# fp32r transposes of P, one pair later, from a copy that GpSimd issues

## The chip, the cores and the metric

One NeuronCore of a Trainium2 chip runs the whole program as one launch. The metric is the device time of that core in microseconds. The kernel before takes 1619.56 us, the median of three runs (1619.38 to 1620.76).

## What is computed

A transformer layer of 1024 tokens plus 16 meta tokens, model width 1024, all in float32: a mixer of retention (4 heads) and sliding-window attention (16 query heads, 4 key heads of 64), then an MLP of width 4096. The part that matters here is the attention over blocks of 128 queries. Each block sees 16 meta keys, the block before and its own; each head has a sink that takes part in the softmax alone.

```python
def block(args):
    qn, kn, vn, n = args
    ...
    keys = jnp.concatenate([k_meta, kn], axis=1)
    vals = jnp.concatenate([v_meta, vn], axis=1)
    scores = (jnp.einsum('bqhgd,bkhd->bhgqk', qn, keys).astype(jnp.float32)
              - slopes * dist.astype(jnp.float32))
    scores = jnp.where(valid, scores, -jnp.inf)
    m = jnp.maximum(jnp.max(scores, axis=-1, keepdims=True), sink)
    p = jnp.exp(scores - m)
    probs = p / (jnp.sum(p, axis=-1, keepdims=True) + jnp.exp(sink - m))
    return jnp.einsum('bhgqk,bkhd->bqhgd', probs.astype(vals.dtype), vals)
```

## The kernel before

Every engine has its own program, written out by hand; semaphores join them. Large products are split in a high and a low part of type fp32r and done as three matmuls (high x high, high x low, low x high: lines 1084, 1088, 1089). ScalarE casts the high part of each weight tile (WH), VectorE subtracts for the low part (WL, L2172).

The attention is the stage from about 461 to 728 us. Its work is cut into 64 pairs of heads: block n = pair // 8, heads 2p and 2p + 1 with p = pair % 8. It is a software pipeline of STEPS = 67 steps T. TensorE fills the steps with the gate projection (`gate_step`, 3 or 4 triples of matmuls a step), so that it has work while a pair goes through the other engines. A pair's way:

- TensorE, step T: `scores(T)` (L1370), two matmuls of 272 columns (144 in block 0) for each of the two heads, into banks 2 and 3.
- VectorE: `top(T)` (L2630) adds the distance term, writes to PR and finds the maxima NM. PR has three buffers, T % 3, of 546 columns: a sink column, the 272 keys of each head, a sink column.
- ScalarE: the exponential, in place in PR, with its sum in RS (L1932). VectorE: RC = 1 / RS (L2663).
- GpSimd: PR times RC (L959), one instruction for each head; it also writes the two sink columns of the pair to come (`set_sink`, L940).
- TensorE, step T + 2: `transpose_p` (L1384, and L1387 for the meta keys): five transposes of 128 columns from PR, type fp32, to banks 4 and 6; three in block 0. They stand ahead of that step's scores, and ahead of the transposes of the next block's queries and keys (L1419, L1427), which are of type fp32r already.
- ScalarE casts the bank to PTH (L1909), VectorE's `lo_p` makes PTL (L2638) and, every second pair, PTM (L2642). `lo_p` of the pair of two steps ago stands ahead of `top(T)` in VectorE's program.
- TensorE, every second step: `values(G)` for two pairs (L1402, L1406); ScalarE copies the result to YA, SP writes one half of it to RT and GpSimd adds the other (L980, accumulating transfers).

GpSimd's queue also stores the gate tiles (L884), loads KV (L893) and the distances (L968). An instruction that issues a transfer waits for its semaphores in the queue, with all that stands behind it.

Of the kernel before, what the change touches and what calls it, by code (L numbers as in the profile page):

```python
# [14 lines left out]
P = 128  # L15
# [48 lines left out]
STEPS = NPAIR + 3  # L64
# [64 lines left out]
KV_FREE = {4: (6, 7), 5: (0, 7), 6: (0, 1)}  # L129
# [78 lines left out]
def build(nc, x, meta, g_mix, w_in, g_ret, g_q, g_k, sinks, w_ret, w_swa, w_out, g_mlp, w_up, w_down,  # L208
          c_ident, c_mask, c_cols, c_dist, x_ch, g_ch, out):
    with ExitStack() as ctx:  # L210
# [92 lines left out]
        KV = at("KV", O_M, [NB, SL])  # L303
        KVR = at("KVR", O_M, [NB, SL], F32R)
        MKV = at("MKV", O_M + 16384, [SL])
        MVB = at("MVB", O_M + 18432, [2, 4 * P], F32R)
        KST = at("KST", O_M + 22528, [2, 4, P], F32R)
        KNF = at("KNF", O_M + 26624, [256])
        PTH = at("PTH", O_M + 27776, [2, 4, P], F32R)
# [3 lines left out]
        RSW = at("RSW", O_M + 31872, [NB, 20])  # L313
# [8 lines left out]
        YA = [at("YA0", O_V + 30208, [SL]), at("YA1", O_M + 16384, [SL])]  # L322
        YA2 = at("YA2", O_M + 22528, [SL])
# [58 lines left out]
        def kv_half(tile, n, c):  # L382

            return tile[:, n, :].rearrange("p (g c d) -> p g c d", g=4, c=2)[:, :, c, :]
# [194 lines left out]
        GS0, CF0, MU0 = 4, 48, 64  # L579

        raw_aside = [*xb_full, *yc_done]

        def raw_block(slab, k):
# [6 lines left out]
            if k in (4, 5) and slab in KV_FREE:  # L590
                return KV[:, KV_FREE[slab][k - 4], :]
# [14 lines left out]
        def _(sp):  # L606
# [84 lines left out]
            for T in range(STEPS):  # L691
# [3 lines left out]
                elif T == 23:  # L695
                    sp.wait_ge(pv_full, 8)
                    sp.wait_ge(w_ready, wn(SLAB_D + 1, 5) + 1)
                    load_aside(SLAB_D + 2)
                elif T == 41:
                    sp.wait_ge(pv_full, 12)  # L700
# [102 lines left out]
        def _(pool):  # L803
# [139 lines left out]
            pool.wait_ge(d_set, 1)  # L943
            set_sink(0)
# [6 lines left out]
            for T in range(STEPS + 2):  # L951
                if T + 1 < NPAIR:
                    set_sink(T + 1)
                if 1 <= T <= NPAIR:
# [21 lines left out]
                if T >= 6 and T % 2 == 0:  # L976
                    G = (T - 6) // 2
# [100 lines left out]
        def _(pe):  # L1078
# [281 lines left out]
            def scores(T):  # L1360
                n, p = T // 8, T % 8
                g = p // 2
                if p % 2 == 0:
                    pe.wait_ge(aqT_rdy, 4 if n == 0 else 4 * n + g + 1)
                    pe.wait_ge(akT_rdy, 4 if n == 0 else 4 * n + g + 1)
                for hl in range(2):
                    if T >= 1:
                        pe.wait_ge(nm_rdy, 2 * (T - 1) + hl + 1)
                    for part in range(2):
                        mm = pe.matmul(B[2 + hl][:, 0:NKEY if n else NKEY0], QT[:, 2 * p + hl, :], KTS[:, part, g, keys_of(n, hl)],  # L1370
                                       start=part == 0, stop=part == 1)
                    mm.then_inc(sc_full, 1)

            def transpose_p(pair):
                n, b = pair // 8, pair % 3
                pe.wait_ge(pn_rdy, pair + 1)
                if pair >= 1:
# [1704 lines left out]
```

## Time and profile before

| | |
|---|---|
| median of three runs | 1619.56 us |
| lowest, highest | 1619.38, 1620.76 us |
| span of the profiled execution | 1618.2 us, 22594 instructions |
| busy over the span | TensorE 99%, VectorE 64%, ScalarE 48%, GpSimd 27% |

The page gives the profiled execution's span, from its first to its last instruction; no time of its own for the whole execution stands beside it, so the 1.3 us between span and median hold what lies around the span and the difference from run to run. A row of the timeline reads: start in us from the span's start, duration, engine, line, operation, output <- inputs, shapes, count of merged instructions, and in brackets how long the engine had been idle and who released it. PE is TensorE's matmuls, PEld its weight loads, DVE VectorE, ACT ScalarE, POOL GpSimd. Matmuls are pipelined: the distance from start to start is what one costs. A row of POOL begins when the instruction is handed over, so behind a running one its duration holds the wait.

### The profile page before, as it was taken

What the parts mean: (1) busy time and instruction counts of PE and PEld (TensorE: products, weight loads), DVE (VectorE), ACT (ScalarE), POOL (GpSimd) and SP (SyncE); (2) the same over time, 40 slices, a digit from 0 to 9 for tenths busy, and PEclk for the clock granted to TensorE, in tenths of its full rate; (3) what the DMA queues carried; (4) which work ended last, traced back from release to release, by engine and by line L of the source; (5) the groups of instructions that cost most, each with busy time, mean ns of one, the idle gap of its engine ahead of it and who ended that gap; (6) DMA issues with size and microseconds to landing.
All of it is one profiled execution on the core that took longest, in us unless ns stands there. A gap on an engine that the chain in (4) does not pass through costs nothing.

```text
span 1618.2 us, 22594 instructions
## 1 busy us (share of the span) xinstructions
PE 1610.1 (99%) x7984; PEld 1347.5 (83%) x7984; DVE 1030.6 (64%) x1913; ACT 769.9 (48%) x1567; POOL 437.1 (27%) x675
## 2 busy tenths in 40 slices
PE   9999999999999999999999999999999999999999
PEld 6888888888888888888888888888888888888887
DVE  6775556655657676757565338866665657766675
ACT  6533334545547676763222126655545544444442
POOL 1101010221359888875221000121111122100000
PEclk9999999999999999999999999999999999999999
DMA  8323232645424343438553223344444399733452
GB/s 289 116 98 117 95 124 72 232 166 186 162 88 114 84 94 83 106 82 262 164 202 104 72 65 124 129 170 150 149 144 148 119 321 356 239 98 98 149 183 92
DMA packets 119599, 236.53 MB, mean 146 GB/s; under 512 B 13904, under 2 KB 48128, under 8 KB 119488
## 3 DMA queue, kind: packets, MB, share of 16 engines
q0 software_dynamic: 45904, 126.93, 23.6%
q1 hardware_dynamic: 73440, 108.03, 21.6%
q8 instruction: 64, 1.05, 0.3%
q14 instruction: 47, 0.39, 0.1%
q10 hardware_dynamic: 144, 0.13, 0.0%
HBM read 157.05 MB, written 69.47 MB: 140 GB/s over the span
## 4 chain that ended last, share of the span: by engine, by line
PE 97%; DVE 1%; DMA 1%; ACT 0%; SPq 0%; POOL 0%; issue 0%; DVEq 0%; ACTq 0%
PE bank L1084 29%; PE bank L1089 29%; PE bank L1088 29%; PE bank L1370 2%; PE bank L1402 2%; PE bank L1384 2%; PE bank L1419 0%; PE bank L1127 0%; PE bank L1502 0%; PE bank L1288 0%; PE bank L1406 0%; PE bank L1452 0%; DMA PX<-in_w_in 0%; PE bank L1387 0%; DVE WL L2172 0%; PE bank L1427 0%
## 5 line engine op out<-in xcount | busy, mean ns | idle before, releaser
L1084 PE MATMUL bank<-WH,ADH 128*128 128x512 f32 x448 | 174.3, 389 | 0.0
L1088 PE MATMUL bank<-WH,ADL 128*128 128x512 f32 x448 | 174.3, 389 | 0.0
L1089 PE MATMUL bank<-WL,ADH 128*128 128x512 f32 x448 | 174.3, 389 | 0.0
L1084 PE MATMUL bank<-HN,WH 128*128 128x512 f32 x384 | 152.4, 397 | 0.0
L2098 ACT CAST ADH<-ARAW 128x512 fp32r<-128x512 f32 x112 | 69.5, 621 | 169.9 <-PE bank L1089 160.9
L1089 PE MATMUL bank<-HN,WH 128*128 128x512 f32 x384 | 150.3, 391 | 0.0
L1088 PE MATMUL bank<-HN,WL 128*128 128x512 f32 x384 | 150.0, 391 | 0.0
L959 POOL TENSOR_SCALAR PR<-PR,RC 128x272 f32<-128x272 f32 (+1 forms) x128 | 131.0, 1099 | 44.9 <-DVE RC L2663 44.4
L2917 DVE TENSOR_TENSOR ADL<-ARAW,ADH 128x512 fp32r<-128x512 f32 x112 | 77.5, 692 | 96.9 <-ACT ADH L2098 96.7
L1084 PE MATMUL bank<-SOPH,WH 128*128 128x512 f32 x256 | 99.8, 390 | 0.0
L1089 PE MATMUL bank<-SOPL,WH 128*128 128x512 f32 x256 | 99.6, 389 | 0.0
L1088 PE MATMUL bank<-SOPH,WL 128*128 128x512 f32 x256 | 99.6, 389 | 0.0
L1088 PEld LDWEIGHTS bank<-WH,ADL 128*128 128x128 f32 x448 | 84.1, 188 | 17.6
L1089 PEld LDWEIGHTS bank<-WL,ADH 128*128 128x128 f32 x448 | 84.1, 188 | 17.4
L1084 PEld LDWEIGHTS bank<-WH,ADH 128*128 128x128 f32 x448 | 84.1, 188 | 17.4
L1932 ACT ACTIVATE PR<-PR,NM 128x273 f32<-128x273 f32 (+1 forms) x128 | 64.4, 506 | 50.1 <-DVE NM L2630 50.1
L1089 PEld LDWEIGHTS bank<-HN,WH 128*128 128x128 f32 x384 | 72.0, 188 | 15.8
L1084 PE MATMUL bank<-WH,HN 128*128 128x512 f32 x208 | 82.7, 397 | 1.1 <-DVE WL L2172 0.7
L1084 PEld LDWEIGHTS bank<-HN,WH 128*128 128x128 f32 x384 | 72.3, 188 | 12.3 <-issue 0.3
L1088 PEld LDWEIGHTS bank<-HN,WL 128*128 128x128 f32 x384 | 72.3, 188 | 11.9
L1089 PE MATMUL bank<-WL,HN 128*128 128x512 f32 x208 | 81.1, 390 | 0.0
L1088 PE MATMUL bank<-WH,HN 128*128 128x512 f32 x208 | 81.0, 390 | 0.0
(356 smaller groups left out, 4242.8 us busy)
## 6 DMA issues: line engine op xcount, KB each, us to landing
ARAW<-uop SPq DMA_DIRECT2D x112, 256.0 KB, 3.0
uop<-US POOLq DMA_DIRECT2D x64, 256.0 KB, 2.8
WRAW<-in_w_up SPq DMA_DIRECT2D x15, 1024.0 KB, 6.2
RAW<-in_w_in SPq DMA_DIRECT2D x58, 256.0 KB, 4.0
gates<-TB POOLq DMA_DIRECT2D x48, 256.0 KB, 2.4
uop<-UA POOLq DMA_DIRECT2D x48, 256.0 KB, 3.1
proj<-SA POOLq DMA_DIRECT2D x36, 256.0 KB, 2.5
RT<-proj POOLq DMA_DIRECT2D x8, 1024.0 KB, 8.8
```

The source lines that it names most:

```text
L959: pr = pool.tensor_scalar(keys, keys, RC[:, b, hl:hl + 1], None, ALU.mult)
L1084: mm = pe.matmul(bank, ahi, bhi, start=first, stop=False, skip_group_check=onto)
L1088: pe.matmul(bank, alo, bhi, start=False, stop=False, skip_group_check=onto)
L1089: return pe.matmul(bank, ahi, blo, start=False, stop=last, skip_group_check=onto)
L1370: mm = pe.matmul(B[2 + hl][:, 0:NKEY if n else NKEY0], QT[:, 2 * p + hl, :], KTS[:, part, g, keys_of(n, hl)], start=part == 0, stop=part == 1)
L1384: pe.transpose(B[4][:, c * P:(c + 1) * P], PR[:, b, key:key + P], IDN[:, :])
L1402: pe.matmul(B[7][:, :], v, tile[:, sl, :, :].rearrange("p h t -> p (h t)"), start=opens, stop=True, skip_group_check=not opens)
L1932: e = act.activation(part, part, ACT.Exp, scale=-1.0, bias=NM[:, T % 3, hl:hl + 1], accum_out=RS[:, T % 3, hl:hl + 1])
L2098: act.copy(ADH[:, n % 4, :], ARAW[:, n % 4, :]).then_inc(da_hi, 1)
L2917: dve.tensor_tensor(ADL[:, n % 4, :], ARAW[:, n % 4, :], ADH[:, n % 4, :].bitcast(F32), ALU.subtract)\
```

## The change

PW is a new tile of two buffers, type fp32r. When GpSimd has scaled pair T - 1 it issues a transfer within SBUF that copies the 544 key columns of PR to PW (144 x 2 in block 0); its waits are its own scaling (`pn_rdy`) and the transposes of the pair two before (`pt_full`). TensorE transposes from PW, in type fp32r with the fp32r identity IDR, at step T + 3 (LAG = 3), one transpose behind each score matmul and the fifth behind the last. Values, and the high and low parts of P, move a step later with it; STEPS is 68. The sink columns are written by VectorE, just ahead of the maxima, once the copy of the pair that used the buffer has landed. To make room, KV keeps four blocks instead of eight, loaded later, and two RAW blocks lie in an area of their own, RAWA, so SP loses two waits.

```diff
+LAG = 3
-STEPS = NPAIR + 3
+STEPS = NPAIR + LAG + 1
...
-KV_FREE = {4: (6, 7), 5: (0, 7), 6: (0, 1)}
+ASIDE = (4, 5, 6)
+NKV = 4
...
-        KV = at("KV", O_M, [NB, SL])
+        KV = at("KV", O_M, [NKV, SL])
+        RAWA = at("RAWA", O_M + 8192, [2, SL])
+        PW = at("PW", O_M + 12288, [2, 2 * NKEY], F32R)
...
-                if T >= 4 and T % 2 == 0:
-                    G = (T - 4) // 2
+                if T >= LAG + 2 and T % 2 == 1:
+                    G = (T - LAG - 2) // 2
                     sp.wait_ge(ya_rdy, G + 1)
...
-            def set_sink(T):
-
-                if T >= 3:
-                    pool.wait_ge(e_rdy, T - 2)
-                p = T % 8
-                first, second = sink_at(T // 8, 0), sink_at(T // 8, 1)
-                pool.tensor_copy(PR[:, T % 3, first:second + 1:second - first], NSK[:, 2 * p:2 * p + 2]).then_inc(sk_set, 1)
+            def copy_p(pair):
+
+                n, b = pair // 8, pair % 2
+                lo, hi = (0, 2 * NKEY) if n else (P, P + 2 * NKEY0)
+                if pair >= 2:
+                    pool.wait_ge(pt_full, pair - 1)
+                pool.wait_ge(pn_rdy, pair + 1)
+                pool.dma_start(PW[:, b, lo:hi].bitcast(F32), PR[:, pair % 3, 1 + lo:1 + hi]).then_inc(pw_full[b], 16)
...
                     pr.then_inc(pn_rdy, 1)
+                    copy_p(T - 1)
...
-                if T in (5, 13, 21, 37):
-                    n = min(T // 8, 3)
-                    pool.wait_ge(qh_rdy, 3 * n + 3 if n else 2)
+                if T % 8 == 4 and 2 <= T // 8 < 6:
+                    n = T // 8 - 2
+                    pool.wait_ge(pv_full, 4 * (n + 2))
                     pool.wait_ge(qf_rdy, n + 2)
-                    if n >= 2:
-                        pool.wait_ge(w_ready, wn(SLAB_D + n - 1, 5) + 1)
-                    load_kv(n + 4)
+                    load_kv(n + NKV)
...
+            def transpose_p(pair, c):
+                n, b = pair // 8, pair % 2
+                if c == 0:
+                    pe.wait_ge(pw_full[b], PW0[b] + 16 * (pair // 2 + 1))
+                    if pair >= 1:
+                        pe.wait_ge(pl_rdy, split_of(pair - 1))
+                    else:
+                        pe.wait_ge(aqT_rdy, 4)
+                if c == 4:
+                    if pair % 2 == 0 and pair >= 2:
+                        pe.wait_ge(pl_rdy, meta_of(pair // 2 - 1))
+                    pe.transpose(B[6][:, (pair % 2) * P:(pair % 2 + 1) * P].bitcast(F32R),
+                                 PW[:, b, 2 * P:3 * P], IDR[:, :]).then_inc(pt_full, 1)
+                elif c // 2 in slots_of(n):
+                    key = pr_slot(n, c % 2, c // 2) - 1
+                    pe.transpose(B[4][:, c * P:(c + 1) * P].bitcast(F32R), PW[:, b, key:key + P], IDR[:, :])
...
-                if T >= 4 and T % 2 == 0:
-                    values((T - 4) // 2)
-                if 2 <= T < NPAIR + 2:
-                    transpose_p(T - 2)
+                if T >= LAG + 2 and T % 2 == 1:
+                    values((T - LAG - 2) // 2)
...
-                if T < NPAIR:
-                    scores(T)
+                for i in range(5):
+                    if T < NPAIR and i < 4:
+                        score(T, i)
+                    if LAG <= T < NPAIR + LAG:
+                        transpose_p(T - LAG, i)
...
                 if T >= 3:
-                    dve.wait_ge(pt_full, T - 2)
+                    dve.wait_ge(pw_full[(T - 3) % 2], PW0[(T - 3) % 2] + 16 * ((T - 3) // 2 + 1))
+                if T == 0:
+                    dve.wait_ge(d_set, 1)
+                first, second = sink_at(n, 0), sink_at(n, 1)
+                dve.tensor_copy(PR[:, T % 3, first:second + 1:second - first], NSK[:, 2 * p:2 * p + 2]).then_inc(sk_set, 1)
```

`score(T, i)` is one of the four matmuls of `scores(T)`, with the same waits.

TensorE, the middle of the stage (step 27, fourth block), before: the gate's matmuls, then the transposes of pair 25 from PR, then the four scores of pair 27.

```order
L1089 MATMUL bank<-HN,WH 128x512
L1384 MATMUL bank<-IDN,PR 128x128 [waits pl_rdy,pn_rdy]
L1384 MATMUL bank<-IDN,PR 128x128 x3
L1387 MATMUL bank<-IDN,PR 128x128
L1370 MATMUL bank<-KTS,QT 128x272 [waits nm_rdy]
L1370 MATMUL bank<-KTS,QT 128x272
L1370 MATMUL bank<-KTS,QT 128x272 [waits nm_rdy]
L1370 MATMUL bank<-KTS,QT 128x272
L1084 MATMUL bank<-HN,WH 128x512
```

The same step of the change (the semaphore named c_full is one of the two that PW's copies count on, which are shared with earlier uses):

```order
L1406 MATMUL bank<-PTM,MVB 128x2x128
L1368 MATMUL bank<-KTS,QT 128x272 [waits nm_rdy]
L1388 MATMUL bank<-IDR,PW 128x128 [waits pl_rdy,c_full]
L1368 MATMUL bank<-KTS,QT 128x272
L1388 MATMUL bank<-IDR,PW 128x128
L1368 MATMUL bank<-KTS,QT 128x272 [waits nm_rdy]
L1388 MATMUL bank<-IDR,PW 128x128
L1368 MATMUL bank<-KTS,QT 128x272
L1388 MATMUL bank<-IDR,PW 128x128
L1384 MATMUL bank<-IDR,PW 128x128 [waits pl_rdy]
L1084 MATMUL bank<-HN,WH 128x512
```

The transposes, of pair 24 now, stand behind one score each, the last two next to each other; this step now has the values ahead of them.

GpSimd at about the same steps, before:

```order
L940 COPY PR<-NSK 128x2 [waits e_rdy]
L959 TENSOR_SCALAR PR<-PR,RC 128x272 [waits rc_rdy]
L959 TENSOR_SCALAR PR<-PR,RC 128x272
L884 DMA gates<-TB 128x512 [waits a_free]
L980 DMA RT<-YA_154 64x2x128 [waits yc_done0]
L980 DMA RT<-YA_154 64x2x128
```

and of the change, over two steps, in one of which KV is loaded:

```order
L960 TENSOR_SCALAR PR<-PR,RC 128x272 [waits rc_rdy]
L960 TENSOR_SCALAR PR<-PR,RC 128x272
L945 DMA PW<-PR 128x544 [waits pn_rdy,pt_full]
L980 DMA RT<-YA_156 64x2x128 [waits yc_done0]
L980 DMA RT<-YA_156 64x2x128
L960 TENSOR_SCALAR PR<-PR,RC 128x272 [waits rc_rdy]
L960 TENSOR_SCALAR PR<-PR,RC 128x272
L945 DMA PW<-PR 128x544 [waits pn_rdy,pt_full]
L897 DMA KV<-proj 128x4x64 [waits qf_rdy,pv_full]
L897 DMA KV<-proj 128x4x64
```

The sink copy is gone and the copy of P stands right behind the scaling, ahead of the step's other transfers.

## Rows read from the trace of the kernel before

**Rows 1.** The page: busy time and share of each engine; TensorE's clock by slice.

```profile
PE 1610.1 (99%) x7984; PEld 1347.5 (83%) x7984; DVE 1030.6 (64%) x1913; ACT 769.9 (48%) x1567; POOL 437.1 (27%) x675
...
PEclk9999999999999999999999999999999999999999
```

**Rows 2.** The chain of waits that ended last, by engine.

```profile
PE 97%; DVE 1%; DMA 1%; ACT 0%; SPq 0%; POOL 0%; issue 0%; DVEq 0%; ACTq 0%
```

**Rows 3.** Busy us by engine in the attention stage, 461 to 728, eight stretches summed.

```profile
sum 267.00, PE 266.52 PEld 231.75 DVE 183.84 ACT 183.76 POOL 219.13; mean PE 33.31 PEld 28.97 DVE 22.98 ACT 22.97 POOL 27.39
```

**Rows 4.** Groups of TensorE instructions: the transposes of P, busy us, mean ns.

```profile
L1384 PE MATMUL bank<-IDN,PR 128*128 128x128 f32 x240 | 36.7, 273 | 0.5 <-POOL PR L959 0.5
...
L1387 PE MATMUL bank<-IDN,PR 128*128 128x128 f32 x64 | 17.4, 273 | 0.0
```

**Rows 5.** Timeline of TensorE's matmuls, one step.

```profile
566.31 0.60 PE L1384 MATMUL bank<-IDN,PR 128*128 128x128 f32 x4
566.75 0.27 PE L1387 MATMUL bank<-IDN,PR 128*128 128x128 f32 x1
...
567.36 0.39 PE L1084 MATMUL bank<-HN,WH 128*128 128x512 f32 x1
```

**Rows 6.** Timeline of weight loads, fp32r transposes of queries.

```profile
453.69 1.42 PEld L1337 LDWEIGHTS bank<-IDR,QST 128*128 128x128 f32 x16 [0.54 <-DVE KTS L2589]
455.06 0.19 PEld L1084 LDWEIGHTS bank<-HN,WH 128*128 128x128 f32 x1
```

**Rows 7.** Timeline of weight loads, fp32r matmuls of 128 columns.

```profile
303.42 1.08 PEld L1288 LDWEIGHTS bank<-QTR,KTR 128*128 128x128 f32 x8
304.43 0.19 PEld L1084 LDWEIGHTS bank<-HN,WH 128*128 128x128 f32 x1
```

**Rows 8.** Groups of GpSimd instructions in the stage, 461 to 728.

```profile
L980 POOL DMA_DIRECT2D RT<-YA x60 | 61.6, 1227 | 0.0
L940 POOL COPY PR<-NSK 128x2 f32<-128x2 f32 x63 | 43.6, 693 | 0.0
...
L893 POOL DMA_DIRECT2D KV<-proj x8 | 7.6, 1121 | 0.0
```

**Rows 9.** Lines 884 and 980 in the stage: ns min/median/max, then landing from issue.

```profile
L884 POOL DMA_DIRECT2D gates<-TB x26: 612/636/1365, 468.1 to 719.0; - x26
...
DMA to landing us min/median/max: 2.4/2.7/4.8
...
L980 POOL DMA_DIRECT2D RT<-YA x60: 972/1330/2174, 482.1 to 723.7; - x60
...
DMA to landing us min/median/max: 2.5/3.2/6.3
```

**Rows 10.** Timeline of all engines, pair 31 on its way, and step 32.

```profile
584.47 0.27 PE L1387 MATMUL bank<-IDN,PR 128*128 128x128 f32 x1
...
584.71 0.73 PE L1370 MATMUL bank<-KTS,QT 128*128 128x272 f32 x4
...
586.57 0.50 DVE L2630 CUSTOM_DVE_ANT_0 PR<-bank,DT,NSK 128x272 f32<-128x272 f32 x1
...
588.60 1.91 POOL L959 TENSOR_SCALAR PR<-PR,RC 128x272 f32<-128x272 f32 x2 [1.88 <-DVE RC L2663]
...
588.92 0.27 PE L1387 MATMUL bank<-IDN,PR 128*128 128x128 f32 x1
...
590.46 0.49 DVE L2630 CUSTOM_DVE_ANT_0 PR<-bank,DT,NSK 128x272 f32<-128x272 f32 x1
...
597.48 0.74 PE L1370 MATMUL bank<-KTS,QT 128*128 128x272 f32 x4
```

**Rows 11.** Timeline of VectorE and GpSimd, a scaling behind weight splits, a sink copy.

```profile
567.85 1.27 DVE L2172 TENSOR_TENSOR WL<-RAW,WH 128x512 fp32r<-128x512 f32 x2
...
568.03 2.79 POOL L959 TENSOR_SCALAR PR<-PR,RC 128x272 f32<-128x272 f32 x2
...
570.78 0.18 POOL L940 COPY PR<-NSK 128x2 f32<-128x2 f32 x1
```

More of the change, by code:

```diff
@@ L579, in build @@
         GS0, CF0, MU0 = 4, 48, 64
+        pw_full, PW0 = [c_full, mu_full], [CF0 + 48, MU0 + 64]
         raw_aside = [*xb_full, *yc_done]
@@ L1358, in _, with score @@
                     ahead[i]()
-            def scores(T):
-                n, p = T // 8, T % 8
+            def score(T, i):
+                n, p, hl, part = T // 8, T % 8, i // 2, i % 2
                 g = p // 2
-                if p % 2 == 0:
+                if p % 2 == 0 and i == 0:
                     pe.wait_ge(aqT_rdy, 4 if n == 0 else 4 * n + g + 1)
                     pe.wait_ge(akT_rdy, 4 if n == 0 else 4 * n + g + 1)
[L1366 to L1371, printed above, removed]
-                    mm.then_inc(sc_full, 1)
@@ L1374, in transpose_p @@
[L1374 to L1377, printed above, removed]
-                    pe.wait_ge(pl_rdy, split_of(pair - 1))
-                else:
-                    pe.wait_ge(aqT_rdy, 4)
-                for sl in slots_of(n):
-                    for hl in range(2):
-                        c, key = 2 * sl + hl, pr_slot(n, hl, sl)
-                        pe.transpose(B[4][:, c * P:(c + 1) * P], PR[:, b, key:key + P], IDN[:, :])
-                if pair % 2 == 0 and pair >= 2:
-                    pe.wait_ge(pl_rdy, meta_of(pair // 2 - 1))
-                pe.transpose(B[6][:, (pair % 2) * P:(pair % 2 + 1) * P],
-                             PR[:, b, 1 + 2 * P:1 + 3 * P], IDN[:, :]).then_inc(pt_full, 1)
+                if T >= 1 and part == 0:
+                    pe.wait_ge(nm_rdy, 2 * (T - 1) + hl + 1)
@@ new lines, in score @@
+                mm = pe.matmul(B[2 + hl][:, 0:NKEY if n else NKEY0], QT[:, 2 * p + hl, :], KTS[:, part, g, keys_of(n, hl)],
+                               start=part == 0, stop=part == 1)
+                if part == 1:
+                    mm.then_inc(sc_full, 1)
+            def transpose_p(pair, c):
[14 more added lines that the diff above has]
+                    pe.transpose(B[4][:, c * P:(c + 1) * P].bitcast(F32R), PW[:, b, key:key + P], IDR[:, :])
@@ L1941, in _ @@
                         g.then_inc(a_free if c < 16 else th_rdy, 1)
-                if 2 <= T < NPAIR + 2:
-                    take_p(T - 2)
-                if T >= 4 and T % 2 == 0:
-                    take_y((T - 4) // 2)
+                if LAG <= T < NPAIR + LAG:
+                    take_p(T - LAG)
+                if T >= LAG + 2 and T % 2 == 1:
+                    take_y((T - LAG - 2) // 2)
                 if T % 8 == 2 and T // 8 + 1 < NB:
@@ L2675, in _ @@
                         split_lo(slab, k)
-                if T > NPAIR:
+                if T > NPAIR + 1:
                     for slab, k in new_slabs(T):
                         split_lo(slab, k)
-                if T >= NPAIR and T < NPAIR + 2:
+                if NPAIR + 1 <= T < NPAIR + 3:
                     for b in range(4):
-                        lo_ys(4 * (T - NPAIR) + b, b, T - NPAIR)
-                splits = new_slabs(T) if T < NPAIR else []
+                        lo_ys(4 * (T - NPAIR - 1) + b, b, T - NPAIR - 1)
+                splits = new_slabs(T) if T <= NPAIR else []
                 if T % 8 == 0 and T // 8 + 1 < NB:
```

52 lines of the change are left out of this document (23 added, 29 removed).

## The prediction

> **What bounds the kernel now.** I read the page's busy shares first, then the chain of waits, then the busy time by stretch. TensorE is busy 99% of the span and the clock row shows 9 in every slice, so the granted clock never falls [rows 1]. The chain that ended last is 97% TensorE [rows 2]. In the stage that the change touches, 461 to 728 us, TensorE is busy 266.52 of 267 us, while GpSimd is busy 219.13, VectorE 183.84 and ScalarE 183.76 [rows 3]. So nothing is won unless TensorE itself does less, and anything that makes TensorE wait there costs its full length. The second thing to see is that GpSimd is at 82% of that stage already; no other helper is nearly so full. The sum is made against the span of the profiled execution, 1618.2 us; the median of the runs is 1.3 us above it, which I add at the end. A measurement of this kernel can tell a change from none at about 0.2%, 3.2 us.
>
> **TensorE's own work.** The change touches 240 + 64 = 304 transposes [rows 4]. Five of them and the four score matmuls of a step are seen in [rows 5]: four transposes from 566.31 to 566.75, 0.109 us each; the whole group of nine takes 567.36 - 566.31 = 1.05, so 5 x 0.109 leaves 0.125 for a score matmul of 272 columns. What an fp32r transpose costs next to another is in [rows 6]: 16 weight loads from 453.69 to the next load at 455.06, 0.0855 each. That looks like 304 x 0.0235 = 7.1 us. But the new order doesn't put them next to each other. It puts four of the five behind a score matmul, with another score matmul behind each. What counts is then which of matmul and following weight load is the longer. The weight load of an ordinary fp32r matmul is in [rows 7]: eight from 303.42 to 304.43, of which the first sat behind a matmul of 512 columns (0.23), so 0.78 / 7 = 0.111 each, although those matmuls have only 128 columns. A transpose streams 128 columns too, so it can't cover the 0.111 of the score matmul's load behind it. Score, transpose: 0.125 as now, the load of the transpose is hidden. Transpose, score: 0.111, where the fp32 transpose costs 0.109. Only the fourth transpose, followed by the fifth, gets 0.0855. So a group of nine falls from 1.05 to about 1.02. That is 0.024 x 56 pairs with five transposes, 1.3 us; the eight pairs of the first block (three transposes) and the last three pairs, which have no scores beside them, bring 0.4. Together **-1.7 us**. The transposes of the next block's queries and keys keep their neighbours: 0.
>
> The page "TensorE: Matmul & The Clock Gate" of the Trainium skill (section on LDWEIGHTS) gives a load as columns / 1.2, 107 ns for 128 columns, for every kind. The trace agrees for the ordinary load (0.111) and not for the transposes (0.0855). By that rule alone a transpose would cost 0.107 everywhere and this term would be -0.6 us instead of -1.7; the measured rows decide.
>
> **GpSimd.** Removed: 64 copies of two sink columns, about 0.2 us each by their shortest (0.18, [rows 11]); the 43.6 us of [rows 8] is mostly waiting behind transfers that are still being issued. Added: 64 issues of a transfer of 128 rows of 2176 bytes. The nearest row is the gate store, 128 rows of 2048 bytes, 0.636 us [rows 9]; the other end is the accumulating transfer of y, 1.03 us for each of a pair ([rows 8]: 61.6 us over 60). I take the gate store, nearly the same shape. 219.1 - 64 x 0.2 + 64 x 0.63 = 246.6 us of 267, 92%. By itself that still fits, with 0.3 us to spare in a mean step of 4.17 us. But its work is bunched: a step with scaling (1.9), P's copy (0.63), two y transfers (2.06) and a gate store (0.63) is 5.2 us, and in four steps two loads of KV of about 1 us each come on top (7.6 us over 8, [rows 8]), in others the distances. It then falls 1 to 3 us behind and catches up by 0.3 a step. Copying to PW also waits for the transposes of two pairs earlier; those end about 5.2 us after the pair's own scores began, when its scaling ends as well, so I cost that at nothing. Behind that wait stand the gate stores and the y transfers; their readers are many us away.
>
> **From the scores to the copy.** Now the scores of pair 31 start at 584.71, 0.24 behind the last transpose of that step, VectorE's maxima at 586.57, the scaling runs 588.60 to 590.51 [rows 10]. After the change the last transpose of a step starts some 0.9 us after the first score instead of 0.24 before it, and ScalarE's cast and VectorE's low part stand ahead of the maxima, so these and all behind move by about 1.15: scaled at 591.7. Landing is 2.7 us from the issue (gate store, median; 2.4 to 4.8 [rows 9]): 594.4. TensorE wants it behind the first score three steps on, 597.48 + 0.12 [rows 10]. Slack 3.2 us, less what GpSimd is behind. Where 1 to 3 us of lateness meet a landing in its upper half, it is gone, and what is late next is P. I count six such places (the KV loads, the block ends, the last pairs, where steps are shorter and no score covers the wait), 0.5 us each: **+3.0 us**. Bounds: 0, if landings stay at 2.4 to 2.7 (TensorE waits for P 0.5 us once today [rows 4]); 13, if every copy is late by 0.2. VectorE's added copy (under 0.2 us as on GpSimd) hides in its 83 idle us. The maxima free the score banks: in a step without PTM's low part they started 590.46 - 588.92 = 1.54 after the last transpose [rows 10], so the first is done 0.9 + 1.54 + 0.5 = 2.95 after the first score, and the next scores come no earlier than 3.3 (1.02 for the group, nine gate matmuls at 0.23, two transposes of keys). Fits by 0.35; I put +0.2 there. The KV and RAW buffers move, with loads several steps ahead of use: 0. SP loses two waits: 0. The gate's matmuls are spread over 68 steps instead of 67, same count: 0.
>
> Sum: 1618.2 - 1.7 + 3.0 + 0.2 = 1619.7, and 1.3 to the median: **1621.0 us**.
>
> **Rivals.**
> (a) *The transposes get their cheap rate after all.* If a score's load can be drawn further ahead than behind the transpose, all 304 cost 0.0855 or less, and P arrives in time: 1619.6 - 7.1 = 1612.5. For it: the queue of loads isn't fully visible. Against it: in [rows 7] no load was ever hidden behind a shorter matmul. And an even shorter step would find GpSimd full. Chance 0.12.
> (b) *GpSimd becomes the bound: slower.* It decides when an issue of P's copy costs over (265 - 206.3) / 64 = 0.92 us, with 265 for the stage less 1.7 and 206.3 for GpSimd's work without the sinks. At the 1.03 of the y transfers it is 206.3 + 65.9 = 272.2 us of work in a stage of 265, 7 us over, and some 2 us of waits for RC that it can't fill: 1621 - 3 + 9, about 1628. For: it is the y transfers that share the queue. Against: the gate store's shape. 0.15.
> (c) *Landings come late.* The new transfers add some 17 MB (278 KB a pair) to the queue that carries y, gates and KV, and the y transfers already show a median of 3.2 and a worst of 6.3 us from issue [rows 9]. One copy in four late by 0.7 is 16 x 0.7 = 11 us in place of 3: about 1628. Related: the scaling takes 2.79 us instead of 1.91 when it starts while VectorE splits weights [rows 10, 11]. Chance 0.21. [...]
> (d) *It does nothing visible*: work and waits both near 0, 1619.6. This lies inside the forecast.
>
> **How the numbers follow.** Forecast with (d), 0.52; (a) 0.12; (b) 0.15; (c) 0.21. Faster by over 0.2% is (a) and a sliver of the forecast, 0.13; slower (b) and (c), 0.36; within 0.2% 0.51. The range takes the forecast's bounds, both slow rivals and the near edge of (a): 1614 to 1630. The forecast's own range is 1617 to 1623.
>
> **What would show it.** Right: a group of four scores and five transposes at about 1.02 us, with some 0.11 from each transpose to the score behind it; GpSimd near 245 us in the stage; its issue of P's copy about 0.63; a few TensorE waits on P's transfer, 3 us together; maxima 1 us later in their step. Wrong: groups of 0.95 or less (a), issues near 1 us and GpSimd without idle time (b), waits on the transfer in every other step (c), or waits of the scores for the maxima in most steps, which I hold for nearly free.

## The result, and the profile after

The changed kernel takes **1661.88 us**, the median of four runs (1660.92 to 1662.71), against 1619.47 for the kernel before in the same runs: a ratio of 1.0258, interval 1.0243 to 1.0272. It is 42 us slower where 1621.0 was forecast, and beyond every rival. The profiled execution took 1662.05 us for a span of 1660.1.

The page of the changed kernel: busy time and share, TensorE's busy tenths in 40 slices, and the chain that ended last.

```profile
PE 1620.5 (98%) x7984; PEld 1352.3 (81%) x7984; DVE 1039.0 (63%) x1977; ACT 771.7 (46%) x1567; POOL 472.2 (28%) x675
...
PE   9999999999999888899999999999999999999999
...
PE 87%; POOL 7%; DMA 3%; issue 1%; DVE 1%; ACT 0%; SPq 0%; POOLq 0%; DVEq 0%
```

The holes lie in the attention stage alone, and GpSimd, which had no part in the chain before [rows 2], has 7% of it now. The stage by stretches (length, busy us of TensorE, its weight loads, VectorE, ScalarE, GpSimd, then the granted clock, DMA share, GB/s), cut so that the sum covers the stage to its new end:

```profile
461.00:494.00 33.00, 33.00 (x191) 28.27 (x189) 22.22 (x82) 22.32 (x68) 20.19 (x30) 1.00 0.43 125
494.00:527.00 33.00, 29.42 (x171) 25.17 (x171) 19.05 (x65) 19.35 (x53) 28.59 (x34) 1.00 0.49 132
527.00:560.00 33.00, 28.66 (x171) 24.66 (x170) 19.43 (x63) 18.96 (x50) 28.49 (x33) 1.00 0.49 124
560.00:593.00 33.00, 25.95 (x138) 21.91 (x137) 21.51 (x61) 19.82 (x50) 29.30 (x31) 0.90 0.54 144
...
659.00:692.00 33.00, 26.42 (x144) 22.48 (x143) 22.20 (x63) 19.25 (x50) 28.17 (x31) 0.90 0.53 146
...
sum 309.00, PE 276.23 PEld 235.91 DVE 192.70 ACT 185.95 POOL 256.59; mean PE 30.69 PEld 26.21 DVE 21.41 ACT 20.66 POOL 28.51
```

Against [rows 3] the stage takes 309 us where it took 267: 42 us, the whole loss. TensorE idles 309 - 276.2 = 33 us in it (0.5 before), and is busy 276.2 - 266.5 = 10 us longer for work that should be shorter; two stretches show a granted clock of 0.90. The waits of this stage (engine and line, what it waited for: us, times, longest):

```profile
ACT PTH L1910 <- PE bank L1384: 70.0, 58, 4.3
...
PE bank L1388 <- DMA PW<-PR: 31.2, 19, 4.2
POOL PW L945 <- POOL PR L960: 30.8, 52, 0.8
...
POOL PR L960 <- DVE RC L2668: 9.2, 8, 3.3
POOL PW L945 <- PE bank L1384: 7.5, 12, 0.8
...
POOL gates L888 <- DVE TB L2663: 3.3, 1, 3.3
...
PE bank L1368 <- DVE NM L2635: 0.9, 2, 0.7
```

TensorE's missing 31 us are waits for the copy of P. GpSimd used to be idle until the reciprocals came (44.4 us, 38 times, in the same view of the kernel before); now only 9.2, 8 times. In its place stands an idle time that didn't exist: 30.8 + 7.5 = 38.3 us ahead of its own copy, 64 times. GpSimd's account closes on the stage: 256.6 busy + 38.3 + 9.2 + 3.3 = 307.4 of 309. Of the 9.2 us, 8.2 lie before 494 us, in the first block; behind it GpSimd has nearly nothing left. GpSimd's groups in the stage (count | busy us, mean ns | idle before; the mean holds time queued behind another issue), and six of its rows (start, us):

```profile
L945 POOL DMA_DIRECT2D PW<-PR x64 | 39.4, 615 | 38.4 <-POOL PR L960 30.8 <-PE bank L1384 7.5
L888 POOL DMA_DIRECT2D gates<-TB x27 | 15.3, 567 | 3.6 <-DVE TB L2663 3.3
```

```profile
599.09 1.75 POOL L960 TENSOR_SCALAR PR<-PR,RC 128x272 f32<-128x272 f32 x1
601.44 0.64 POOL L945 DMA_DIRECT2D PW<-PR  x1 [0.60 <-POOL PR L960]
602.11 1.92 POOL L960 TENSOR_SCALAR PR<-PR,RC 128x272 f32<-128x272 f32 x2
604.70 0.61 POOL L945 DMA_DIRECT2D PW<-PR  x1 [0.67 <-POOL PR L960]
605.31 0.55 POOL L888 DMA_DIRECT2D gates<-TB  x1
605.85 2.09 POOL L980 DMA_DIRECT2D RT<-YA  x2
```

The scaling ends at 602.11 + 1.92 = 604.03 and the copy starts at 604.70, though the copy's other wait, for the transposes, was satisfied by then. The gate store behind it, whose own wait (`a_free`) is satisfied too, follows at once. So the issue is 0.62 us as forecast, and the pair pays (39.4 + 38.4) / 64 = **1.22 us**. The views of issues give the copy's landing as 2.0/2.4/5.4 us (minimum, median, maximum): not late by itself.

### The profile page after: what moved, and what is told of

Same layout as the page of the kernel before. It is cut to its first block, busy times and chain, and to the rows that moved or that the text cites. A ratio compares the mean times of both kernels' runs of the same rounds, so it can differ in the third digit from the quotient of the medians.

```text
span 1660.1 us, 22666 instructions
## 1 busy us (share of the span) xinstructions
PE 1620.5 (98%) x7984; PEld 1352.3 (81%) x7984; DVE 1039.0 (63%) x1977; ACT 771.7 (46%) x1567; POOL 472.2 (28%) x675
## 4 chain that ended last, share of the span: by engine, by line
PE 87%; POOL 7%; DMA 3%; issue 1%; DVE 1%; ACT 0%; SPq 0%; POOLq 0%; DVEq 0%
PE bank L1084 27%; PE bank L1089 27%; PE bank L1088 27%; POOL PR L960 4%; DMA PW<-PR 2%; POOL RT L980 2%; PE bank L1368 1%; POOL PW L945 1%; PE bank L1402 1%; PE bank L1388 1%; PE bank L1127 0%; PE bank L1503 0%; PE bank L1288 0%; PE bank L1453 0%; DMA XR<-in_x 0%
## 5 line engine op out<-in xcount | busy, mean ns | idle before, releaser
L1084 PE MATMUL bank<-HN,WH 128*128 128x512 f32 x384 | 159.0, 414 | 0.4 <-DVE WL L2173 0.4
L960 POOL TENSOR_SCALAR PR<-PR,RC 128x272 f32<-128x272 f32 (+1 forms) x128 | 152.2, 1427 | 10.2 <-DVE RC L2668 9.2
L1089 PE MATMUL bank<-HN,WH 128*128 128x512 f32 x384 | 151.7, 395 | 0.0
L2643 DVE TENSOR_TENSOR PTL<-bank,PTH 128x512 fp32r<-128x512 f32 (+1 forms) x64 | 42.0, 657 | 80.8 <-ACT PTH L1910 80.8
L1089 PEld LDWEIGHTS bank<-HN,WH 128*128 128x128 f32 x384 | 73.0, 190 | 16.4
L1388 PE MATMUL bank<-IDR,PW 128*128 128x128 f32 x240 | 54.2, 232 | 31.3 <-DMA PW<-PR 31.2
L1088 PEld LDWEIGHTS bank<-HN,WL 128*128 128x128 f32 x384 | 73.6, 192 | 12.2
L1084 PE MATMUL bank<-WH,HN 128*128 128x512 f32 x208 | 82.7, 397 | 0.8 <-DVE WL L2173 0.3
```

The source lines that it names most:

```text
L960: pr = pool.tensor_scalar(keys, keys, RC[:, b, hl:hl + 1], None, ALU.mult)
L1084: mm = pe.matmul(bank, ahi, bhi, start=first, stop=False, skip_group_check=onto)
L1088: pe.matmul(bank, alo, bhi, start=False, stop=False, skip_group_check=onto)
L1089: return pe.matmul(bank, ahi, blo, start=False, stop=last, skip_group_check=onto)
L1388: pe.transpose(B[4][:, c * P:(c + 1) * P].bitcast(F32R), PW[:, b, key:key + P], IDR[:, :])
L2643: dve.tensor_tensor(pair_part(PTL, n, pair), pair_bank(n), pair_part(PTH, n, pair).bitcast(F32), ALU.subtract)\
```

## The experiments

**Theories.** A: GpSimd's time is the loss; a transfer that has to wait for GpSimd's own scaling costs it a start as well as the issue, 1.22 us a pair, and GpSimd is full. Rivals: the later place of the transposes and their order among the scores; VectorE's sink columns; landings and the DMA queue; the delivery of P itself.

The ratios below are to the kernel before as measured beside each run, with medians from 1620.11 to 1620.86 us.

### sp_copy: the copy on another queue

The call leaves GpSimd's loop, where it stood behind the scaling, and ends SyncE's step, with the same two waits; its landing is counted on two other semaphores.

```diff
-                    copy_p(T - 1)
...
+                if 1 <= T <= NPAIR:
+                    copy_p(T - 1)
```

> The changed kernel with one edit: the copy of P to PW is issued by SP, at the end of its step, with the same waits; GpSimd keeps scaling, y, gates and KV. Theory GPSIMD (its queue is the bound: 0.60 us of idling on its own scaling and 0.62 us of issue for each pair, 78 us of its 308): the stage falls back to 264 to 267 us and the time to 1616 to 1622. Theory LANDING (P arrives late because the transfer is slow or queued behind others): still 1640 or more, with waits of the transposes on the transfer. Theory VECTOR (the sink copies and the later maxima hold everything up): stays near 1660.

Measured: 1641.99 us (1640.27 to 1642.32), ratio 1.0132 (1.0117 to 1.0147). GpSimd is free again: it waits for reciprocals, 75.7 us in the stage, 39 times. That gives 20 of the 42 us back, not all of them as theory A had it; 1640 or more with waits on the transfer is what the rival of late landings expected. The waits of TensorE for P are 12.2 us now, 8 of them, and three of these are holes of over 3 us. One of them, in the timelines of SyncE's queue, GpSimd and TensorE:

```profile
488.21 2.14 POOL L962 TENSOR_SCALAR PR<-PR,RC 128x144 f32<-128x144 f32 x2
```

```profile
489.97 0.51 SPq L704 DMA_DIRECT2D PW<-PR  x1
495.92 0.93 SPq L689 DMA_DIRECT2D RAW<-in_w_in  x2
496.95 0.50 SPq L704 DMA_DIRECT2D PW<-PR  x1
```

```profile
501.37 0.37 PE L1389 MATMUL bank<-IDR,PW 128*128 128x128 f32 x1 [3.55 <-DMA PW<-PR]
```

The pair scaled at 488.21 to 490.35 is the one after that copied at 489.97 (a copy is issued only when its scaling is over). It was issued at 496.95, 6.6 us late, behind two weight loads of SyncE's step at 495.92, which wait for VectorE to split the blocks they overwrite. TensorE stood 3.55 us for it. The transposes began 501.37 - 496.95 = 4.4 us behind the issue, a slow landing beside the 3.1 in the median; with the 6.6 us back it would still have been in time.

### sp_grouped: with the transposes side by side

```diff
-                for i in range(5):
-                    if T < NPAIR and i < 4:
-                        score(T, i)
-                    if LAG <= T < NPAIR + LAG:
-                        transpose_p(T - LAG, i)
+                if LAG <= T < NPAIR + LAG:
+                    for i in range(5):
+                        transpose_p(T - LAG, i)
+                if T < NPAIR:
+                    for i in range(4):
+                        score(T, i)
```

(on top of sp_copy)

> As sp_copy, and the five transposes of a step stand together ahead of the four scores, not one behind each. By the weight loads (0.0855 us between transposes, 0.111 only for the last one, where each transpose ahead of a score now costs 0.111) a group of nine falls from 1.02 to 0.95: 0.07 x 61 pairs = 4 us less than sp_copy, 1612 to 1617. Rival: the order is worth nothing, the same time as sp_copy within 1 us.

Measured: 1631.74 us (1630.56 to 1633.95), ratio 1.0068 (1.0051 to 1.0085): 10 us below sp_copy, where 4 were expected, with three large holes still there. So the order costs, in a kernel where P is late as well; how much, the runs with P in time show further down.

### own_wait: the wait alone

The kernel before, and GpSimd waits for its own scaling; no copy.

```diff
                     pr.then_inc(pn_rdy, 1)
+                    pool.wait_ge(pn_rdy, T)
```

> The kernel before, with one added instruction: after each scaling GpSimd waits for its own scaling to be complete. No transfer of P, nothing else changed. If waiting for its own last instruction costs GpSimd 0.6 us by itself, the idle time ahead of the sink copy or the next transfer is 0.5 to 0.6 us in 64 places, GpSimd is at 219 + 38 = 257 of 267 us and the time rises by 0 to 8 us. If the 0.6 us belongs to the issue of a transfer alone, the idle time appears only where a transfer comes next, and the time stays at 1619 to 1621.

Measured: 1619.77 us (one run). GpSimd's waits in the stage:

```profile
POOL PR L959 <- DVE RC L2664: 22.4, 26, 3.1
...
POOL gates L884 <- POOL PR L959: 8.4, 26, 0.5
POOL RT L981 <- POOL PR L959: 6.6, 19, 0.5
```

The idle time comes up in front of transfers, 8.4 / 26 = 0.32 us each for the gate stores; the sink copies that follow such a wait directly, which are computing instructions, start 0.06 us behind it. Here GpSimd had idle time to pay with: its waits for reciprocals fell from 44.4 us to 22.4.

### copy_behind: the copy after the step's other transfers

Still on GpSimd, but behind the step's gate stores and y transfers.

```diff
-                    copy_p(T - 1)
...
+                if 1 <= T <= NPAIR:
+                    copy_p(T - 1)
```

> The changed kernel with the copy of P behind the step's other transfers (gates, distances, KV, y) in GpSimd's program, not ahead of them. Theory GPSIMD: in the steps that have another transfer (about five in eight) the wait for the scaling is covered, so some 0.6 x 40 = 24 us of idling go, and P lands 1 to 3 us later: 1635 to 1650. Theory LANDING: P later by 1 to 3 us makes it worse, over 1665.

Measured: 1645.85 us (one run). The idle time in front of the copy fell from 30.8 to 10.8 us (18 times, where no other transfer covers it), the time by 16. GpSimd has 26.9 us of waits for reciprocals again, and TensorE still waits 16.4 us for P, which now comes later.

### sp_first: SyncE's copy at the head of its step

```diff
             for T in range(STEPS):
+                if 1 <= T <= NPAIR:
+                    copy_p(T - 1)
...
-                if 1 <= T <= NPAIR:
-                    copy_p(T - 1)
```

> sp_copy with one thing moved: SyncE issues the copy of P at the head of its step, ahead of the weight and y transfers of that step, not behind them. Theory A (in sp_copy the copies at the changes of slab were queued on SyncE behind weight loads that wait for VectorE's splits, which are what made the three gaps of 3 to 4 us and the stretches at a granted clock of 0.90 to 0.95 around them): the gaps of 3.55, 3.38 and 3.17 us go, every stretch shows 0.98 or more, and the time falls from 1642 by the 10 us of gaps and some 8 of clock to 1620 to 1626. Theory B (the copy is late because the scaling itself is late, VectorE's reciprocals standing behind its split work at those places): the gaps stay within 1 us of what they were and the time stays at 1638 to 1643. A new cost could come up: the weight loads now wait behind the copy, which waits for the scaling; then VectorE would show waits for RAW blocks.

Measured: **1623.09 us** (1621.63 to 1624.17), ratio 1.0012 (1.0003 to 1.0022). TensorE's waits for P are 0.2 us in the whole stage. The same stretch of sp_copy and of sp_first:

```profile
494.00:527.00 33.00, 29.20 (x156) 24.83 (x156) 18.70 (x63) 17.47 (x47) 23.31 (x26) 0.90 0.45 124
```

```profile
494.00:527.00 33.00, 32.15 (x190) 27.58 (x189) 21.96 (x73) 20.84 (x57) 27.13 (x29) 1.00 0.55 145
```

With the hole the granted clock is 0.90 and 156 matmuls get done, without it 1.00 and 190. The new wait that was feared (weight loads behind the copy) doesn't show. So everything above 1623 in the changed kernel comes from which queue issues the copy, and when: 1661.9 - 1623.1 = 39 us.

### lag_only and sinks_dve: the rest of the change, without the copy

lag_only keeps the later place, the order among the scores, the smaller ring of KV and VectorE's sink columns, with fp32 transposes straight from PR:

```diff
-                    pe.wait_ge(pw_full[b], PW0[b] + 16 * (pair // 2 + 1))
+                    pe.wait_ge(pn_rdy, pair + 1)
...
-                    pe.transpose(B[4][:, c * P:(c + 1) * P].bitcast(F32R), PW[:, b, key:key + P], IDR[:, :])
+                    pe.transpose(B[4][:, c * P:(c + 1) * P], PR[:, pair % 3, key:key + P], IDN[:, :])
```

> The changed kernel without the copy of P: the transposes are plain fp32 again and read P itself, but a pair later and between the scores, and the sink columns are VectorE's; the ring of four K/V buffers, the aside buffers and the odd steps of y stay too. If the loss of the change is the copy's alone (GpSimd's transfer issues and the waits behind them): within 4 us of before, 1616 to 1624. If the later place or VectorE's sink columns carry a part of it: that part shows here, up to 1645.

Measured: 1622.88 us (1622.09 to 1624.62), ratio 1.0011 (1.0002 to 1.0021): 2 us of the 42.

sinks_dve is the kernel before with `set_sink` moved from GpSimd into VectorE's `top`.

> The kernel before with the sink columns written by VectorE ahead of the maxima and by nothing else. VectorE gets 64 copies of 0.2 to 0.4 us, GpSimd loses 64 of 0.2 us. By the prediction +0.2 us; if the maxima come so much later that TensorE's scores wait, 2 to 10 us more.

Measured: 1619.67 us (one run). No cost; VectorE's 63 copies are 12.9 us of busy time beside TensorE's work.

### lag_group and sp_first_group: order and kind

The grouping of sp_grouped on top of lag_only and of sp_first.

> lag_only with the five plain fp32 transposes together ahead of the scores. Against sp_first_group it differs in the kind of transposes alone (and the copy that fp32r needs). If the rate of a weight load of fp32r transposes next to each other is what sp_first_group won: 1615.9 + 304 x 0.0235 = 1623. If it won by the order, with the kind of no weight: 1616 to 1618.

> sp_grouped (the five transposes together ahead of the scores) with the copy at the head of SyncE's step. A: sp_grouped's 1632 less its gaps of 3.2, 4.7 and 5.3 us and the lower clock around them, 1613 to 1618, which is below the 1619.5 of before. B: stays at 1628 to 1633.

Measured: lag_group 1618.31 us (1617.36 to 1619.09), ratio 0.9988 (0.9978 to 0.9997); sp_first_group **1615.92 us** (1615.43 to 1617.08), ratio 0.9970 (0.9958 to 0.9982), faster than both kernels. Grouping alone, with the plain fp32 kind, is 1.9 us of that (lag_group). The four kernels differ in the order and in the kind (with the copy that fp32r needs), and one step without values of each shows them on TensorE's timeline. Grouped fp32, grouped fp32r, alternating fp32, alternating fp32r:

```profile
502.99 0.63 PE L1378 MATMUL bank<-IDN,PR 128*128 128x128 f32 x4
...
504.07 0.39 PE L1074 MATMUL bank<-HN,WH 128*128 128x512 f32 x1
504.30 0.39 PE L1078 MATMUL bank<-HN,WL 128*128 128x512 f32 x1
```

```profile
503.69 0.51 PE L1389 MATMUL bank<-IDR,PW 128*128 128x128 f32 x4
504.03 0.25 PE L1385 MATMUL bank<-IDR,PW 128*128 128x128 f32 x1
...
504.70 0.40 PE L1085 MATMUL bank<-HN,WH 128*128 128x512 f32 x1
504.93 0.40 PE L1089 MATMUL bank<-HN,WL 128*128 128x512 f32 x1
```

```profile
503.78 0.36 PE L1358 MATMUL bank<-KTS,QT 128*128 128x272 f32 x1
...
504.00 0.38 PE L1358 MATMUL bank<-KTS,QT 128*128 128x272 f32 x1
...
504.83 0.47 PE L1074 MATMUL bank<-HN,WH 128*128 128x512 f32 x1
505.14 0.39 PE L1078 MATMUL bank<-HN,WL 128*128 128x512 f32 x1
```

```profile
504.95 0.36 PE L1369 MATMUL bank<-KTS,QT 128*128 128x272 f32 x1
505.15 0.22 PE L1389 MATMUL bank<-IDR,PW 128*128 128x128 f32 x1
505.21 0.34 PE L1369 MATMUL bank<-KTS,QT 128*128 128x272 f32 x1
505.39 0.22 PE L1389 MATMUL bank<-IDR,PW 128*128 128x128 f32 x1
505.45 0.34 PE L1369 MATMUL bank<-KTS,QT 128*128 128x272 f32 x1
...
505.99 0.46 PE L1085 MATMUL bank<-HN,WH 128*128 128x512 f32 x1
506.29 0.40 PE L1089 MATMUL bank<-HN,WL 128*128 128x512 f32 x1
```

From the first of the nine to the second gate matmul (the first is drawn long after a transpose): 1.31, 1.24, 1.36, 1.34 us; over all groups of nine in the stage that are followed by a gate matmul and have no idle time (some fifty in each kernel) the means are 1.30, 1.22, 1.36 and 1.33. Side by side the fp32r kind is worth 0.07 here; alternating it is worth 0.02. In the last fence score to score is 505.45 - 505.21 = 0.24 us: 0.18 to the transpose and 0.06 back. The alternating order costs 0.05 for fp32 and 0.10 for fp32r. In run times the fp32r kind wins nothing alternating (1623.1 against 1622.9 for fp32, within the spread) and 2.4 us grouped (1615.9 against 1618.3), where I had expected 7 from 304 x 0.0235. TensorE is busy 4.9 us less in that run (1604.6 against 1609.5 over the span); its waits for P, 1.7 us in three places, are a part of what was lost again. The order is worth 4.6 us for fp32 and 7.2 for fp32r. Where lag_group is one side of a difference, the kernels before differ by 0.6 us, so 4.6 may be 4.0 and 2.4 may be 3.0.

### extra, extra_two, extra_wait: GpSimd's price by itself

sp_first, where P arrives by SyncE, and GpSimd issues one or two transfers more a pair which nothing reads, from a tile that nothing changes. The first added line stands in extra_wait alone, the third in extra_two alone.

```diff
                     pr.then_inc(pn_rdy, 1)
+                    pool.wait_ge(pn_rdy, T) 
+                    pool.dma_start(spare[T - 1], HN[:, 0, 0, 0:2 * NKEY].bitcast(F32)).then_inc(c_full, 16)
+                    pool.dma_start(spare[NPAIR + T - 1], HN[:, 0, 0, 0:2 * NKEY].bitcast(F32)).then_inc(c_full, 16)
```

> sp_first (SyncE copies P) plus one more transfer a pair that nothing reads, issued by GpSimd right behind its scaling: 128 rows of 2176 bytes from a tile that nothing changes to a spare place in memory. It waits for nothing. GpSimd is busy 209.5 of 267 us in sp_first's stage; 64 x 0.62 makes 249, so by both theories it still fits and the time stays within 5 us of sp_first's 1623. If queues and landings were what the copy on GpSimd spoils, this run would already be slow (over 1630).

> As extra, with two such transfers a pair and no wait: 1.24 us of issue a pair. If what counts is GpSimd's time alone, wherever it comes from, this is as slow as extra_wait (1643 to 1662); by the prediction's own bound an issue cost over 0.92 us a pair makes GpSimd the limit. If the wait hurts in another way (the order of releases), this one stays near 1625.

> As extra, but GpSimd first waits for the semaphore of its own scaling, as the copy of P has to. Theory A (a transfer's issue that waits for the scaling can't begin under it and starts 0.6 us behind its end, so the pair costs 1.22 us of GpSimd instead of 0.62): 209.5 + 64 x 1.22 = 288 us of work for a stage of 267, so the stage grows by 20 us or more and the time is 1643 to 1662. Theory B (the issue's 0.62 is all that counts and the change lost elsewhere): the same time as extra.

Measured: extra 1630.67 us (1628.11 to 1631.24), ratio 1.0062 (1.0045 to 1.0079); extra_wait 1650.30 (1647.65 to 1652.49), 1.0181 (1.0166 to 1.0196); extra_two 1657.88 (1655.75 to 1659.44), 1.0228 (1.0213 to 1.0243). One pair of extra and one of extra_two on GpSimd's timeline, then the transfer's group in extra_wait:

```profile
603.25 1.90 POOL L963 TENSOR_SCALAR PR<-PR,RC 128x272 f32<-128x272 f32 x2 [0.57 <-DVE RC L2671]
605.11 0.60 POOL L966 DMA_DIRECT2D spare<-HN  x1
605.71 2.10 POOL L983 DMA_DIRECT2D RT<-YA  x2
```

```profile
600.14 1.16 POOL L966 DMA_DIRECT2D spare<-HN  x1
600.74 1.10 POOL L967 DMA_DIRECT2D spare<-HN  x1
601.27 1.10 POOL L900 DMA_DIRECT2D gates<-TB  x1
```

```profile
L967 POOL DMA_DIRECT2D spare<-HN x64 | 39.9, 623 | 20.4 <-POOL PR L963 20.4
```

Without a wait the issue joins the scaling without a gap (603.25 + 1.90 = 605.15) and costs 0.60 us, two of them 601.27 - 600.14 = 1.13; with one wait it costs (39.9 + 20.4) / 64 = 0.94. Extra was slower than expected (7.6 us over sp_first where 5 was the bound, just past the 1630 that I had set for queues), and extra_wait, at +27 us, is where theory A wanted it. Extra_two, without any wait, is slower still: what counts is the engine's time, wherever it comes from. But it moves twice the extra bytes as well, so it speaks against the queue only together with extra_wait, which moves the same bytes as extra and costs 20 us more. Whether the bytes have a part in extra's own 7.6 us, no run separates.

### extra_wait_2: what the second wait does

In extra_wait the start is 0.32 us, in the changed kernel 0.60. In the changed kernel two waits stand ahead of the copy, in extra_wait one. So a second was added, on a semaphore reached long before:

```diff
+                    pool.wait_ge(rc_rdy, T)
                     pool.wait_ge(pn_rdy, T)
```

> extra_wait with a second wait ahead of the transfer, on a semaphore that has long been reached (the reciprocals'). In the changed kernel two waits stand ahead of the copy of P (the transposes of two pairs earlier, its own scaling) and it starts 0.60 us behind the scaling; in extra_wait one wait stands there and it starts 0.32 behind. Theory A2 (each wait ahead of a transfer costs about 0.3 us of GpSimd): the start is 0.60 again, the pair costs 1.22 us as in the changed kernel, and the time rises from extra_wait's 1650 to 1657 to 1664. Theory B2 (the 0.60 is something of the copy of P itself, such as its source or the transposes it waits for): the start stays at 0.32 and the time at 1648 to 1652.

Measured: 1660.18 us (1659.51 to 1660.83), ratio 1.0248 (1.0233 to 1.0263). The group:

```profile
L968 POOL DMA_DIRECT2D spare<-HN x64 | 39.9, 623 | 39.0 <-POOL PR L963 37.1 <-DVE RC L2673 2.0
```

39.0 / 64 = 0.61 us of start, though the added wait is already satisfied.

It is not 0.3 us for each wait, though: GpSimd's other transfers contradict that. In the kernel before, 51 transfers of the stage stand directly behind a scaling (26 gate stores, 19 pairs of y transfers, 3 of KV, 3 of the distances), each with a wait for another engine that is satisfied, and all start without a gap. In own_wait the same transfers have that wait and the one for the scaling, and most start 0.30 us behind. What differs is where the trace has the wait for the scaling. In own_wait and extra_wait it is part of the transfer's instruction: a median start of 0.30. In 62 copies of the changed kernel (L944) and all 64 of extra_wait_2 (L967) it is a semaphore instruction by itself, done about 0.05 us behind the scaling's end, and the transfer behind it carries the satisfied wait: a median start of 0.60 and 0.59. The first two copies of the changed kernel have no wait for transposes, and start 0.30 behind. In all these runs the first of two waits in the program went into the transfer's instruction and the second stood by itself, so the two waits of `copy_p` the other way round might start at 0.30; that was not tried.

extra_wait_2 delivers P by SyncE and doesn't use what GpSimd copies, and is as slow as the changed kernel within 2 us, with GpSimd as busy in the stage (256.5 us against 256.6): GpSimd's time is enough for the loss, and P needn't pass through its queue.

### copy_next: the copy a step later on GpSimd

```diff
             for T in range(STEPS + 2):
+                if 2 <= T <= NPAIR + 1:
+                    copy_p(T - 2)
                 if 1 <= T <= NPAIR:
...
-                    copy_p(T - 1)
```

> The changed kernel with GpSimd's copy of P moved from behind its own scaling to the head of GpSimd's next step, ahead of the wait for the next reciprocals: the scaling it needs is long over, so by A its issue costs 0.62 us and no start, partly inside idle time. GpSimd then has 209.5 + 40 = 250 us of work and fits again: 1622 to 1632, the upper end if the copy, some 3 to 4 us later, lands behind the third step's scores here and there. By B (the copy costs what it costs on GpSimd, or it comes too late anyway): 1650 or more.

Measured: 1643.54 us (1638.59 to 1645.54), ratio 1.0136 (1.0118 to 1.0153). A miss by 11.5 us above my upper end. The start was not gone as I thought: 12.4 us in front of the copy are left of 38.4, nearly all in the 19 places where no other transfer stands between a scaling and the copy. Behind another transfer 42 copies, with the same two waits, start without a gap. And TensorE waits 16.2 us for a P that is now issued later. GpSimd has 23.7 us of waits for reciprocals. It is better than the changed kernel by 18 us and needs nothing from another queue. How its 20 us over sp_first divide between GpSimd's time and the later issue, no run tells.

In order of GpSimd's added time for a pair, all against sp_first's 1623.1: 0.60 us +8, 0.94 +27, 1.13 (the two issues of extra_two) +35, 1.22 (extra_wait_2) +37, and the changed kernel, 1.22, +39.

## Why the prediction was wrong

**The step that failed** is in GpSimd's part: "Copying to PW also waits for the transposes of two pairs earlier; those end about 5.2 us after the pair's own scores began, when its scaling ends as well, so I cost that at nothing", and the sum beside it, 64 x 0.63 for the copies. I asked when the awaited events come, and there I was right: the transposes were the late one only 12 times. The wait for GpSimd's own scaling isn't priced there at all: I didn't ask what a wait costs GpSimd when nothing is late. Shown by own_wait, extra_wait and extra_wait_2: a transfer that waits for the scaling just ahead of it starts 0.3 us late, and 0.6 where a second wait stands with it as in the copy, 38.4 us over 64 pairs. With 1.22 in place of 0.63 my own sum gives 206.3 + 64 x 1.22 = 284.4 us of work for a stage of 265, and so at least 19 us.

**Rival (b)** was the right mechanism, at a chance of 0.15, with the wrong price (about 1628; its own sum gives 1627). Its decision point (0.92 us) took GpSimd's time as one pool. Extra shows that the loss begins below it: 0.60 a pair costs 8 us while GpSimd still waits 24.3 us for reciprocals in extra's stage. That its idle time can't all be filled is the likely reason; the added bytes are not excluded. And above the decision point the price isn't the excess alone: in the changed kernel TensorE idled 33 us and was busy 10 longer. The two stretches with its longest waits for P, 4.2 us, show a granted clock of 0.90; those of 494 to 560 us, with shorter ones that add to 3.6 and 4.3 us, stay at 1.00.

**GpSimd's busy time.** Forecast 246.6 us, measured 256.6. The issues were right (0.615 us against 0.63). Of the remaining 10 us about 9 lie in the scaling: 130 us in place of 122, when each row counts only from the end of the one ahead of it. Most pairs of 272 columns take 1.91 to 1.95 us, but 13 of 56 take over 2.3 where 3 did before ([rows 11] has one of them, 2.79). All 13 run beside VectorE instructions that work on two tiles of SBUF (splits, the norms of queries and keys), for 0.86 us at least and 1.8 in the mean, against 0.1 for the others. Why they meet more often in the changed kernel, no run tells.

**Late P.** Six places of 0.5 us were forecast, 19 with 31 us came. With the copy in time (sp_first) they are 0.2 us: the slack of 3.2 us was enough, the assumption that GpSimd falls behind by 1 to 3 us and catches up was wrong.

**Landings, rival (c).** The median from issue to landing on GpSimd's queue is 2.4 us in the changed kernel, below the 2.7 that I took. In sp_first the same copies on SyncE's queue land after 1.9/3.0/4.9 us and still come in time. Not the cause.

**TensorE's own work.** The sum held: between scores the fp32r kind doesn't get its cheap rate, 0.240 us for score and transpose where I had worked out 0.236, and nine take 505.99 - 504.95 = 1.04 us where I said 1.02. Rival (a) fell with it. The way there didn't hold. I had 0.125 from a score to the transpose and 0.111 from the transpose to the next score, whose weight load I took as exposed, and named that 0.111 as a sign of being right; the rows show 0.18 and 0.06. The extra time stands ahead of the transposes, and that the sums agree is luck. What I also missed is that the alternation has a price of its own: lag_only against lag_group is 4.6 us for plain fp32. TensorE is busy 1611.6 us over the span of sp_first, against 1610.1 before, so the term came out at about +1.5 in place of -1.7. Part of that stands behind the group, where the first gate matmul takes 0.30 us to the next in place of 0.23.

The page "TensorE: Matmul & The Clock Gate" of the Trainium skill (section on LDWEIGHTS) gives a weight load as columns / 1.2, which is 107 ns for 128 columns, and names no kind. This case doesn't agree for transposes side by side: four grouped fp32r ones take 504.03 - 503.69 = 0.34 us in sp_first_group, 85 ns each, and the grouped runs differ by kind, 1.31 against 1.24 us.

**Maxima and sinks.** Forecast +0.2 and nothing: the scores wait 0.9 us for the maxima in the changed kernel, 1.2 in sp_first, and sinks_dve shows no cost. Small, as forecast.

## What to carry to other kernels

Before you put a transfer behind the work that it depends on, on the same engine's queue, charge the engine the issue and a start (0.3 or 0.6 us here), and add up whether that engine still has idle time that can be filled. Another engine's queue can be a better place, if the transfer stands ahead of whatever blocks there (sp_first against sp_copy); the same copy cost 39 us on one queue and none that could be seen on the other. And the cheaper kind of transposes paid only with its transposes next to each other: keep them together.

## What was not expected of the hardware

- A transfer that GpSimd issues right behind its own work starts without a gap when it awaits nothing (extra) or only another engine's semaphore, long reached (51 transfers of the kernel before). If it waits for that work itself, it starts about 0.3 us behind (own_wait, extra_wait), and 0.61 if that wait is a semaphore instruction by itself (extra_wait_2; 0.60 in the changed kernel). Ahead of computing instructions the gap is 0.06 us (own_wait).
- A hole of 3.55 us in TensorE's work went with a mean granted clock of 0.90 over the 33 us stretch around it, between its levels 1.00 (2.4 GHz) and 0.50 (1.2 GHz); the same stretch without the hole shows 1.00 (sp_copy, sp_first).
- Score matmuls of 272 columns and fp32r transposes of 128, alternating, take 0.18 us from score to transpose and 0.06 back; fp32 transposes in the same place have a longer row (0.27 us against 0.22) and cost nearly the same in sum (1.36 against 1.34 us for the group and the first gate matmul).
